# Two queues for the expert weights: the up matrices are issued by ScalarE, gates and downs by SyncE

## The chip, the cores and the metric

The kernel runs on one core of a Trainium2 chip. The metric is device time in microseconds (us), taken from the start to the end of one execution. The engines of the core are PE (TensorE, matrix products), ACT (ScalarE), DVE (VectorE), POOL (GpSimd) and SP (SyncE, which here only issues transfers). Sixteen DMA engines move data between the memory outside the core (HBM) and SBUF. An engine that issues a DMA only hands over its description; a semaphore counts up when the data have landed.

## The reference

Two layers, each a mixer (left out here: the change touches nothing of it), a layer norm, a mixture of experts, and a second layer norm, on 256 tokens of width 1024, all in float32:

```
def moe(x, router_w, router_bias, w_gate, w_up, w_down, sw_gate, sw_up, sw_down):
    ...                       # 8 of 64 experts per token, with weights wts
    def expert_block(args):
        b_tok, b_w, e = args
        xb = xt[b_tok]
        h = jax.nn.silu(xb @ w_gate[e]) * (xb @ w_up[e])
        return (h @ w_down[e]) * b_w[:, None].astype(xt.dtype)
    ...
    shared = (jax.nn.silu(xt @ sw_gate) * (xt @ sw_up)) @ sw_down
    return (routed + shared).reshape(bsz, s, d)
```

Each of the 64 experts of a layer has three matrices of 1 MB: gate and up (1024 by 256) and down (256 by 1024). Every matrix is read from HBM once per layer, 192 MB for each of the two layers.

## The kernel before

Each engine runs its own program; they meet at semaphores. The program has four stages in a row: mixer 0 (`mix0`), experts 0 (`moe0`), mixer 1, experts 1.

In a stage of experts the 64 experts are taken in 32 **pairs**. Four slots in SBUF (`ew`, `NSLOT` = 4) hold the weights of four experts, so of two pairs: the pair that is being computed and the next one. Pair n uses the slots 2u and 2u+1 with u = n mod 2; the loads for pair n+2 go into the same slots as soon as pair n has let go of them.

PE works through a pair in this order (`pe_moe`, `octets`): it waits until gate and up of both experts have landed (`gu_in`, L1119) and multiplies the gathered tokens by them (L1124, 32 products in 7.1 us; then `gu_full` counts up). It scatters the results of the pair before (L1050), turns the hidden values (L1138), gathers tokens for the next octet of experts (L1079), waits for the downs (`d_in`, L1159) and multiplies by them (L1168; then `y_hi_full` counts up). Four pairs make an octet of experts. In the last octet the gathers are replaced by products of the shared expert (L1086) and of the residual (L1067). After the last pair, L1060 scatters once more and the layer norm follows.

ACT has three tasks in a pair (`act_moe`, `octets`): SiLU of the gate half (L1388, after `gu_full`), a copy of gathered tokens (L1379, after PE's gather; PE's products L1168 wait for it), and the scaled copy of one half of the result (L1392, after `y_hi_full`). DVE does the rest.

SP issues the weights (`sp_moe`, `group`): it waits for `gu_full` of pair n, then issues gate and up of the first expert of pair n+2, gate and up of the second (L308, L309), waits for `y_hi_full` of pair n, and issues the two downs (L413). All go to SP's one queue and are served in that order. The first four experts of a layer are loaded ahead of the loop by `first_load`. After the loop, SP issues the loads of the next stage into the same queue.

Of the kernel before, what the change touches and what calls it, by code (L numbers as in the profile page):

```python
# [18 lines left out]
KC = D // P  # L19
# [4 lines left out]
NE = 64  # L24
# [62 lines left out]
def build(nc, A, out, stages=("mix0", "moe0", "mix1", "moe1")):  # L87
    ctx = ExitStack()
    with ctx:
# [212 lines left out]
                eng.wait_ge(S["h_ready"], TT * (k - 1) + t + 1)  # L302


        def expert_load(sp, m, l, e, s):
            src_g = A["exp_w_gate"][l, e].rearrange("(p c) f -> p (c f)", c=KC)
            src_u = A["exp_w_up"][l, e].rearrange("(p c) f -> p (c f)", c=KC)
            sp.dma_start(ew[:, s, 0:EW], src_g).then_inc(m["gu_in"][s], 16)  # L308
            sp.dma_start(ew[:, s, EW:2 * EW], src_u).then_inc(m["gu_in"][s], 16)  # L309

        def down_src(l, e):
            return A["exp_w_down"][l, e].rearrange("(p j) n -> p (j n)", j=JE)
# [70 lines left out]
        def sp_moe(sp, l):  # L383
# [17 lines left out]
                first_load(sp, m, l, s)  # L401
            sp_ln_params(sp, k, A["ln2_w"][l], A["ln2_b"][l])

            def group(base, it):

                for u in range(2):

                    sp.wait_ge(m["gu_full"], (base - 1) * 2 + u + 1)
                    for s in (2 * u, 2 * u + 1):
                        expert_load(sp, m, l, it * NSLOT + s, s)  # L410
                    sp.wait_ge(m["y_hi_full"], (base - 1) * 2 + u + 1)
                    for s in (2 * u, 2 * u + 1):
                        sp.dma_start(ew[:, s, 2 * EW:3 * EW], down_src(l, it * NSLOT + s)).then_inc(m["d_in"][s], 16)  # L413
# [4 lines left out]
            npass = sp.value_load(npass_i[0:1, 0:1], min_val=1, max_val=MAX_PASS)  # L418
            with sp.If(npass > 1):
                with sp.Fori(1, npass) as ps:  # L420
                    with sp.Fori(0, NE // NSLOT) as it:
                        group(ps * (NE // NSLOT) + it, it)
            return npass

# [938 lines left out]
        def act_moe(act, l, chain):  # L1363
# [18 lines left out]
            def octets(ps, it, last=False):  # L1382
                for v in range(2):
                    for q in range(OCT // 2):
                        u = q % 2
                        n = ps * PAIRS + it * OCT + v * (OCT // 2) + q
                        act.wait_ge(m["gu_full"], n + 1)
                        nc.scalar.activation(sg[:, :], bank[6][:, 0:DE], ACT.Silu).then_inc(m["silu"], 1)  # L1388
                        if not (last and v == 1):
                            gathered(1 - v, 2 * q, n + 5, 4)  # L1390
                        act.wait_ge(m["y_hi_full"], n + 1)
                        nc.scalar.activation(y_top[:, 512:1024], bank[5][:, :], ACT.Copy, scale=slot_gate[:, u:u + 1])\  # L1392
                          .then_inc(m["y_hi"], 1)
# [723 lines left out]
```

## Time and profile before

| what | us |
|---|---|
| median of 3 runs (1257.76 to 1260.94) | 1257.88 |
| the profiled execution | 1257.82 |
| its span, first to last instruction | 1256.1 |
| PE busy | 1166.2 (93% of the span) |
| ACT busy | 193.3 (15%) |
| queue q1 (SP's DMAs) | 462.37 MB, packets cover 90.5% of the time of 16 engines |
| pairs of experts 0 | from 156.32 to about 624 |
| pairs of experts 1 | from 776 to about 1244 |

Times inside the span count from its start. A busy PE says that products were in flight, and not that it ran at its peak. "DMA share" is the part of the time in which the 16 DMA engines had a packet under way; neighbouring packets overlap a little, so that it can read 1.01. "Idle before" names the event that ended an engine's idle time.

### The profile page before, as it was taken

To read this page: it belongs to the slowest core of one execution; us is meant where nothing else is said; L and a number is where in the kernel's file an instruction comes from. 1 tells how busy PE (TensorE), PEld (TensorE's weight loads), DVE (VectorE), ACT (ScalarE), POOL (GpSimd) and SP (SyncE) were. 2 spreads that over 40 slices of the span, in tenths; PEclk is the share of its full clock that TensorE was granted. 3 is DMA by queue.
4 is the path that set the end of the run, shared out by engine and by line. 5 is a ranking of instruction groups with operands and counts; after the bars stand their busy time and mean duration, and the time that the engine had idled before them with its cause. 6 is when DMAs were issued, how large, how long until landed. Compare 5 with 4: busy or idle time off the path is not lost.

```text
span 1256.1 us, 17816 instructions
## 1 busy us (share of the span) xinstructions
PE 1166.2 (93%) x7245; PEld 567.4 (45%) x7245; DVE 489.3 (39%) x1059; ACT 193.3 (15%) x330; POOL 47.3 (4%) x78
## 2 busy tenths in 40 slices
PE   9999999988888888999899999999888988889996
PEld 8774833333333333333387657333333333333332
DVE  5994733332323233332327256332333233232224
ACT  3231311111111111110122312111111111111102
POOL 6200100000000000000000001000000000000000
PEclk9999999999999999999999999999999999999999
DMA  9775989999999999999953278999999999999993
GB/s 347 205 301 193 421 344 422 420 421 421 421 421 422 422 422 422 422 421 421 399 176 134 96 288 340 419 420 422 420 421 422 420 422 422 422 422 421 421 422 154
DMA packets 76125, 463.78 MB, mean 369 GB/s; under 512 B 8544, under 2 KB 9888, under 8 KB 25376
## 3 DMA queue, kind: packets, MB, share of 16 engines
q1 hardware_dynamic: 75920, 462.37, 90.5%
q8 instruction: 47, 0.77, 0.2%
q10 hardware_dynamic: 144, 0.52, 0.1%
q14 instruction: 14, 0.11, 0.0%
HBM read 456.51 MB, written 6.36 MB: 368 GB/s over the span
## 4 chain that ended last, share of the span: by engine, by line
PE 51%; DMA 42%; SPq 3%; DVE 2%; issue 1%; ACT 1%; DVEq 0%; POOL 0%; POOLq 0%
DMA expert_weights<-in_exp_w_up 40%; PE bank L1124 23%; PE bank L1168 5%; PE bank L652 4%; PE bank L638 3%; PE bank L999 2%; PE bank L726 2%; PE bank L742 2%; SPq L308 2%; PE bank L1050 1%; PE bank L753 1%; DMA expert_weights<-s_rows 1%; PE bank L1079 1%; SPq L309 1%; DMA s_rows<-hidden 1%
## 5 line engine op out<-in xcount | busy, mean ns | idle before, releaser
L1124 PE MATMUL bank<-expert_weights,weight_ring 128*64 128x512 f32 x1024 | 226.8, 595 | 30.9 <-DMA expert_weights<-in_exp_w_up 30.9
L1168 PE MATMUL bank<-expert_weights,hiddenT 128*32 128x512 f32 x2048 | 233.0, 595 | 10.0 <-ACT weight_ring L1379 5.0
L1989 DVE TENSOR_TENSOR hidden<-silu_gate,bank 128x256 f32<-128x256 f32 x64 | 27.0, 422 | 424.3 <-ACT silu_gate L1388 424.3
L1124 PEld LDWEIGHTS bank<-expert_weights,weight_ring 128*64 128x64 f32 x1024 | 81.1, 137 | 175.5 <-issue 175.2
L1124 PE MATMUL bank<-expert_weights,hT 128*64 128x512 f32 x512 | 118.4, 603 | 30.7 <-DMA expert_weights<-in_exp_w_up 30.4
L1168 PEld LDWEIGHTS bank<-expert_weights,hiddenT 128*32 128x32 f32 x2048 | 60.0, 109 | 146.0 <-issue 119.4
L1124 PE MATMUL bank<-expert_weights,octet_high 128*64 128x512 f32 x512 | 116.0, 592 | 0.0
L1388 ACT ACTIVATE silu_gate<-bank 128x256 f32<-128x256 f32 x64 | 24.6, 385 | 471.1 <-PE bank L1124 471.1
L2001 DVE TENSOR_SCALAR y_top<-bank,slot_gate 128x512 fp32r<-128x512 f32 x64 | 48.1, 751 | 108.1 <-PE bank L1168 108.1
L1124 PEld LDWEIGHTS bank<-expert_weights,hT 128*64 128x64 f32 x512 | 39.5, 138 | 110.1 <-issue 110.1
L1392 ACT ACTIVATE y_top<-bank,slot_gate 128x512 fp32r<-128x512 f32 x64 | 44.0, 687 | 268.7 <-PE bank L1168 268.7
L1124 PEld LDWEIGHTS bank<-expert_weights,octet_high 128*64 128x64 f32 x512 | 42.6, 137 | 67.2 <-issue 67.2
L2008 DVE SCALAR_TENSOR_TENSOR y_low<-bank,slot_gate,y_top 128x512 fp32r<-128x512 f32 x64 | 48.0, 751 | 57.6 <-ACT y_top L1392 57.6
L1079 PE MATMUL bank<-onehot_r,h_top 128*128 128x256 f32 x256 | 67.8, 300 | 0.0
L638 PE MATMUL bank<-hT,weight_ring 128*128 128x256 f32 x304 | 66.6, 380 | 0.0
L1079 PE MATMUL bank<-onehot_r,h_low 128*128 128x256 f32 x256 | 62.7, 279 | 0.0
L638 PEld LDWEIGHTS bank<-hT,weight_ring 128*128 128x128 f32 x304 | 57.4, 190 | 7.8
L1050 PE MATMUL bank<-y_top,onehotT_r 64*128 64x512 f32 x256 | 57.5, 445 | 0.0
L652 PE MATMUL bank<-weight_ring,hT 128*128 128x512 f32 x128 | 56.2, 594 | 0.1
L1050 PE MATMUL bank<-y_low,onehotT_r 64*128 64x512 f32 x256 | 50.5, 390 | 0.0
L2004 DVE SCALAR_TENSOR_TENSOR y_low<-bank,slot_gate,y_top 128x512 fp32r<-128x512 f32 x64 | 48.1, 751 | 2.3
L1079 PEld LDWEIGHTS bank<-onehot_r,h_top 128*128 128x128 f32 x256 | 48.8, 191 | 0.0
(384 smaller groups left out, 1061.5 us busy)
## 6 DMA issues: line engine op xcount, KB each, us to landing
expert_weights<-in_exp_w_gate SPq DMA_DIRECT2D x128, 1024.0 KB, 15.0
expert_weights<-in_exp_w_up SPq DMA_DIRECT2D x128, 1024.0 KB, 17.1
expert_weights<-in_exp_w_down SPq DMA_DIRECT2D x128, 1024.0 KB, 18.7
weight_ring<-in_w_in_even SPq DMA_DIRECT2D x5, 2048.0 KB, 9.9
weight_ring<-in_w_out SPq DMA_DIRECT2D x4, 2048.0 KB, 7.8
weight_ring<-in_w_in_odd SPq DMA_DIRECT2D x4, 2048.0 KB, 10.5
s_c<-expert_weights SPq DMA_DIRECT2D x1, 3072.0 KB, 9.7
expert_weights<-s_c SPq DMA_DIRECT2D x1, 3072.0 KB, 10.3
```

The costliest lines, as they stand in the source:

```text
L308: sp.dma_start(ew[:, s, 0:EW], src_g).then_inc(m["gu_in"][s], 16)
L638: last = nc.tensor.matmul(B.tile(f"{name}{i}")[:, a * SEQ:(a + 1) * SEQ], w[:, c, (2 * i + a) * P:(2 * i + a + 1) * P], hT[:, c, :], start ...
L652: last = nc.tensor.matmul(B.tile(f"{name}{t}")[:, :], hT[:, c, t * P:(t + 1) * P], w[:, c, :], start=(c == 0), stop=(c == KC - 1))
L1050: nc.tensor.matmul(bank[2 * t + n][:, :], onehotT[slot_rows(t), par, :], part[slot_rows(t), n * 512:(n + 1) * 512], start=False, stop=Fals ...
L1079: last = nc.tensor.matmul(bank[b][:, t * SEQ:(t + 1) * SEQ], part[:, t, c, :], onehot[:, t, :, :].rearrange("p e s -> p (e s)"), start=(pa ...
L1124: last_mm = nc.tensor.matmul(bank[6][a * 2 * CAP:(a + 1) * 2 * CAP, :].rearrange("p (w f) -> p w f", w=2), octet_tokens(l, v, c)[:, 2 * q ...
L1168: last_mm = nc.tensor.matmul(bank[b][by_tile:by_tile + CAP, :], hm[:, j, own:own + CAP], ew_d(2 * u + a)[:, j, half * 512:(half + 1) * 512 ...
L1392: nc.scalar.activation(y_top[:, 512:1024], bank[5][:, :], ACT.Copy, scale=slot_gate[:, u:u + 1])\
L1989: nc.vector.tensor_tensor(hslot[:, :], sg[:, :], bank[6][:, DE:2 * DE], ALU.mult)\
L2001: nc.vector.tensor_scalar(y_top[:, 0:512], bank[4][:, :], slot_gate[:, u:u + 1], None, ALU.mult)\
L2004: nc.vector.scalar_tensor_tensor(out=y_low[:, 0:512], in0=bank[4][:, :], scalar=slot_gate[:, u:u + 1], in1=y_top[:, 0:512], op0=ALU.mult, ...
L2008: nc.vector.scalar_tensor_tensor(out=y_low[:, 512:1024], in0=bank[5][:, :], scalar=slot_gate[:, u:u + 1], in1=y_top[:, 512:1024], op0=ALU. ...
```

## The change

`expert_load` gets a switch for its second transfer, and in the loop SP leaves the ups out. ACT issues them itself: right after its SiLU of pair n it issues the two ups of pair n+2, on its own DMA queue. The semaphores stay the same: `gu_in` of a slot still counts 16 for the gate and 16 for the up, and PE still waits for both. The first four experts of a layer are still loaded whole by SP. Further passes over the experts, which only other inputs would need, keep their first group whole as well.

```
-        def expert_load(sp, m, l, e, s):
+        def expert_load(sp, m, l, e, s, with_up=True):
             src_g = A["exp_w_gate"][l, e].rearrange("(p c) f -> p (c f)", c=KC)
             src_u = A["exp_w_up"][l, e].rearrange("(p c) f -> p (c f)", c=KC)
             sp.dma_start(ew[:, s, 0:EW], src_g).then_inc(m["gu_in"][s], 16)
-            sp.dma_start(ew[:, s, EW:2 * EW], src_u).then_inc(m["gu_in"][s], 16)
+            if with_up:
+                sp.dma_start(ew[:, s, EW:2 * EW], src_u).then_inc(m["gu_in"][s], 16)
...
-            def group(base, it):
+            def group(base, it, with_up=False):
...
-                        expert_load(sp, m, l, it * NSLOT + s, s)
+                        expert_load(sp, m, l, it * NSLOT + s, s, with_up)
...
                         act.wait_ge(m["gu_full"], n + 1)
                         nc.scalar.activation(sg[:, :], bank[6][:, 0:DE], ACT.Silu).then_inc(m["silu"], 1)
+                        if not (last and v == 1 and q >= 2):
+                            for a in range(2):
+                                up = A["exp_w_up"][l, it * 2 * OCT + v * OCT + 2 * q + NSLOT + a]
+                                act.dma_start(ew[:, 2 * u + a, EW:2 * EW], up.rearrange("(p c) f -> p (c f)", c=KC))\
+                                   .then_inc(m["gu_in"][2 * u + a], 16)
                         if not (last and v == 1):
                             gathered(1 - v, 2 * q, n + 5, 4)
```

SP's loop over the pairs of experts 0, before, for one pair (ISA and REGISTER_ALU compute addresses; the names are destination and source of a transfer):

```order
L308 ISA [waits moe0_gu_full]
L308 DMA expert_weights<-in_exp_w_gate 128x2048
L309 DMA expert_weights<-in_exp_w_up 128x2048
L308 ISA
L308 DMA expert_weights<-in_exp_w_gate 128x2048
L309 DMA expert_weights<-in_exp_w_up 128x2048
L413 DMA expert_weights<-in_exp_w_down 128x2048 [waits moe0_y_hi_full]
L413 DMA expert_weights<-in_exp_w_down 128x2048
```

The same place on SP now:

```order
L308 ISA [waits moe0_gu_full]
L308 DMA expert_weights<-in_exp_w_gate 128x2048
L308 ISA
L308 DMA expert_weights<-in_exp_w_gate 128x2048
L414 DMA expert_weights<-in_exp_w_down 128x2048 [waits moe0_y_hi_full]
L414 DMA expert_weights<-in_exp_w_down 128x2048
```

The two ups are gone from between the gates; waits and the rest stand as they did.

ACT at the first two pairs of experts 1, before:

```order
L1388 ACTIVATE silu_gate<-bank 128x256 [waits moe1_gu_full]
L1378 REGISTER_ALU
L1379 COPY hT<-bank 128x2x8x32 [waits moe1_gather_lo]
L1392 ACTIVATE y_top<-bank,slot_gate 128x512 [waits moe1_y_hi_full]
L1388 ACTIVATE silu_gate<-bank 128x256 [waits moe1_gu_full]
```

The same place on ACT now:

```order
L1390 ACTIVATE silu_gate<-bank 128x256 [waits moe1_gu_full]
L1394 DMA expert_weights<-in_exp_w_up 128x2048 x2
L1380 REGISTER_ALU
L1381 COPY hT<-bank 128x2x8x32 [waits moe1_gather_lo]
L1399 ACTIVATE y_top<-bank,slot_gate 128x512 [waits moe1_y_hi_full]
L1390 ACTIVATE silu_gate<-bank 128x256 [waits moe1_gu_full]
```

The two issues stand between SiLU and the copy of gathered tokens and bring no wait of their own. ACT does this for 30 of the 32 pairs of a layer; the last two have nothing more to load.

## Rows read from the trace of the kernel before

**Rows 1.** Page, DMA by 40 slices of the span, and the queues.

```profile
DMA  9775989999999999999953278999999999999993
GB/s 347 205 301 193 421 344 422 420 421 421 421 421 422 422 422 422 422 421 421 399 176 134 96 288 340 419 420 422 420 421 422 420 422 422 422 422 421 421 422 154
...
q1 hardware_dynamic: 75920, 462.37, 90.5%
```

**Rows 2.** Windows in the expert stages: engines' busy us, clock, DMA share, GB/s.

```profile
core 0: us, PE busy (x) PEld busy (x) DVE busy (x) ACT busy (x) POOL busy (x), PEclk, DMA share, GB/s
166.00:176.00 10.00, 9.82 (x62) 3.15 (x64) 3.14 (x5) 0.81 (x2) 0.00 (x0) 1.00 1.01 428
176.00:184.00 8.00, 7.78 (x59) 3.23 (x57) 3.43 (x7) 1.66 (x3) 0.00 (x0) 1.00 1.01 418
200.00:350.00 150.00, 137.91 (x860) 56.80 (x857) 46.34 (x94) 16.97 (x31) 0.00 (x0) 1.00 1.01 421
1000.00:1200.00 200.00, 181.53 (x1122) 75.36 (x1122) 60.15 (x124) 21.55 (x39) 0.00 (x0) 1.00 1.01 422
```

**Rows 3.** Waits over the span, then SP's own: us in total, times, longest.

```profile
PE bank L1124 <- DMA expert_weights<-in_exp_w_up: 61.3, 45, 2.6
...
SPq L308 <- PE bank L1124: 450.9, 60, 24.1
```

**Rows 4.** Timeline of a middle pair: PE, then ACT, then SP.

```profile
311.59 7.09 PE L1124 MATMUL bank<-expert_weights,weight_ring 128*64 128x512 f32 x32 [1.41 <-DMA expert_weights<-in_exp_w_up]
321.45 3.64 PE L1168 MATMUL bank<-expert_weights,hiddenT 128*32 128x512 f32 x32 [0.20 <-ACT octet_high L1379]
326.48 3.65 PE L1124 MATMUL bank<-expert_weights,hT 128*64 128x512 f32 x16 [1.39 <-DMA expert_weights<-in_exp_w_up]
...
318.72 0.39 ACT L1388 ACTIVATE silu_gate<-bank 128x256 f32<-128x256 f32 x1 [7.78 <-PE bank L1124]
320.81 0.59 ACT L1379 COPY octet_high<-bank 128x512 f32<-128x512 f32 x1 [1.71 <-PE bank L1079]
...
318.86 0.33 SPq L308 DMA_DIRECT2D expert_weights<-in_exp_w_gate  x1
319.28 0.38 SPq L309 DMA_DIRECT2D expert_weights<-in_exp_w_up  x1
```

**Rows 5.** Source views of L309 (up) and L308 (gate): issue ns, landing us.

```profile
L309 SPq DMA_DIRECT2D expert_weights<-in_exp_w_up x128: 352/382/792, 119.2 to 1210.3; - x128
DMA to landing us min/median/max: 6.9/17.1/23.5
...
DMA to landing us min/median/max: 4.9/15.0/21.5
```

**Rows 6.** Timeline of the start: the only DMA that ACT issues.

```profile
0.81 0.43 ACTq L1439 DMA_DIRECT2D weight_ring<-in_w_first  x1
```

**Rows 7.** DMA view of 2.5 to 4.5 us: both queues, packets, MB, share.

```profile
DMA packets 256, 0.79 MB, mean 395 GB/s; under 512 B 103, under 2 KB 103, under 8 KB 223
...
q10 hardware_dynamic: 135, 0.49, 61.9%
q1 hardware_dynamic: 121, 0.30, 40.0%
```

**Rows 8.** Timeline of PE, last four pairs of experts 0: start, length, idle before.

```profile
566.56 3.65 PE L1124 MATMUL bank<-expert_weights,hT 128*64 128x512 f32 x16 [0.82 <-DMA expert_weights<-in_exp_w_up]
581.46 3.65 PE L1124 MATMUL bank<-expert_weights,hT 128*64 128x512 f32 x16
596.41 3.65 PE L1124 MATMUL bank<-expert_weights,hT 128*64 128x512 f32 x16
611.44 3.65 PE L1124 MATMUL bank<-expert_weights,hT 128*64 128x512 f32 x16 [1.02 <-DMA expert_weights<-in_exp_w_up]
```

**Rows 9.** The same of experts 1.

```profile
1186.77 3.65 PE L1124 MATMUL bank<-expert_weights,hT 128*64 128x512 f32 x16 [1.16 <-DMA expert_weights<-in_exp_w_up]
1201.56 3.65 PE L1124 MATMUL bank<-expert_weights,hT 128*64 128x512 f32 x16
1216.41 3.65 PE L1124 MATMUL bank<-expert_weights,hT 128*64 128x512 f32 x16
1231.31 3.65 PE L1124 MATMUL bank<-expert_weights,hT 128*64 128x512 f32 x16 [0.89 <-DMA expert_weights<-in_exp_w_up]
```

More of the change, by code:

```diff
@@ L420, in sp_moe @@
                 with sp.Fori(1, npass) as ps:
-                    with sp.Fori(0, NE // NSLOT) as it:
+                    group(ps * (NE // NSLOT), 0, True)
+                    with sp.Fori(1, NE // NSLOT) as it:
                         group(ps * (NE // NSLOT) + it, it)
```

## The prediction

> **What bounds the kernel now.** I read the page's DMA slices first. Through both expert stages the digit is 9, and 28 of the 40 slices stand at 419 to 422 GB/s [rows 1]. The windows say the same in a sharper way: over 150 us of the first expert stage and 200 us of the second the DMA share is 1.01, at 421 and 422 GB/s, while PE is busy 92% and 91% of the time at clock 1.00 [rows 2]. So the DMA engines have no gap there, and PE has some. The waits agree: PE stood 61.3 us in 45 pieces before L1124, all put down to a landing up, at most 2.6 us at once [rows 3]. One middle pair shows the cadence: PE starts L1124 at 311.59 and again at 326.48, so a pair takes 14.89 us, and each start had waited some 1.4 us for the last up [rows 4]. The arithmetic fits: a pair is 6 MB, or 6.29 million bytes, and that at 421 GB/s is 14.9 us. I call a third of it (two gates, two ups or two downs) a **piece** of 4.97 us. The stage is bounded by bytes; the number of issues does not bound it.
>
> SP is no bound. It stood 450.9 us in 60 waits for `gu_full` [rows 3], and what it issues lies in the queue for long: an up lands 17.1 us after its issue in the median, and 6.9 us at least [rows 5].
>
> **The change part by part.**
>
> *SP loses two issues a pair*, 0.38 us each [rows 5], 120 in all. SP waits right afterwards in any case, so this is worth nothing.
>
> *ACT gains two issues a pair.* The trace has one DMA issued by ACT, 0.43 us [rows 6]; SP's ups took 0.35 to 0.79 [rows 5]. ACT has 2.09 us from the start of SiLU (318.72) to the copy L1379 (320.81), SiLU needs 0.39 of it, and 1.71 are idle [rows 4]. Two issues at 0.43 make 0.9 us and fit; even two at 0.79 make 1.6 us and fit. If they did not, the copy would be late, then L1168, and then PE's 1.4 us of waiting before the next pair would have to cover it [rows 4]. I take 0. In the last octet the copy is gone and no cover is needed.
>
> *The bytes stay*, and the first gate of a layer goes out at the same moment as before. With the engines full from there on, the last byte of a layer lands when it did, unless the rate changes. That is the largest open item, since the trace has no stretch in which two queues of large packets are both full. Its bounds are from the nearest rows: 428 GB/s when the stream has just begun and 418 shortly after, against 421 in the long run [rows 2], so +1.7% and -0.7%. I take 0: the share is already 1.01, so there is no bubble between packets for a second queue to fill.
>
> *The order of service changes*, and this is the term that I expect to see. Before, one queue gave gates and ups of pair n, downs of n, gates and ups of n+1, and so on. Now SP's queue holds gates n, downs n, gates n+1, and ACT's holds ups alone. In the only stretch with two queues, both move packets in the same two microseconds, 135 and 121 of them [rows 7]. So they take turns; what share each gets with equal packets this does not settle, and I take half and half. Then the ups run ahead of the gates, which stand behind the downs. How far ahead? Let T be the moment when gates and ups of pair n are both there. Before, everything up to ups n had been served at T. Now gates n come last; everything up to gates n has been served, and on top of it a part of ups n+1. As the engines never rest, T is later by exactly the time of that part.
>
> Ups n+1 are handed over 7.13 us after PE starts pair n-1 (311.59 to 318.72) and a further 0.6 us for SiLU and the issue, so 7.7 us after it [rows 4]. A transfer that nothing stood before took 4.9 us to land [rows 5], of which 2.49 are its 1 MB, so 2.4 us lie around the bytes. Gates n land 0.1 us before PE starts pair n, 14.89 us after the start of n-1. That leaves 14.89 - 7.7 - 2.4 - 0.1 = 4.7 us in which both queues are full, and at half of the turns 2.3 us of ups n+1 are served in it. **T is 2.3 us late**, with 0 and 4.7 us as the ends (no turn, and every turn, for ACT's queue).
>
> In the middle of a stage this costs nothing, as the engines go on. At its end it does: after the last pair there are no ups to run ahead, so the last T is where it was, but PE has to get there. Its last four pairs hardly wait. In experts 0 they start at 566.56, 581.46, 596.41 and 611.44; only the last had waited, 1.02 us [rows 8]. In experts 1 the last had waited 0.89 us and the two before it had no wait [rows 9]. A lateness of 2.3 us at the first of the four goes through all, less that wait: 2.3 - 1.02 = 1.3 us, and 2.3 - 0.89 = 1.4 us. **Sum: +2.7 us**, with ends 0 and (4.7 - 1.02) + (4.7 - 0.89) = 7.5 us.
>
> The downs come later too, but not too late: downs n follow gates n with 4.97 us of their own and share turns with what is left of ups n+1, 2.7 us, so they land 7.7 us after T, and L1168 wants them 9.86 us after the start (311.59 to 321.45) [rows 4]. Cover 2.2 us.
>
> The profiled execution took 1257.82 us, 1.7 more than its span and 0.1 less than the median of the three runs, so the sum can be put on either: 1257.8 + 2.7 = **1260.5 us**.
>
> The Trainium skill (*DMA: Bandwidth & Descriptors*, Queues, rings and completion order) says that each DMA engine goes round its queues packet by packet. The trace agrees as far as it goes, with 135 and 121 packets side by side [rows 7]; by that rule the half is right and the sum is the one above.
>
> **The rivals.** About 0.3% (3.8 us) is what a measurement of this kernel can tell from no change.
>
> *The order stays.* If the engines took the packets roughly as they were issued, or SP's queue got most turns, T would be late by less than 1.02 and 0.89 us, and the waits of the last pair would swallow that: 1257.8 us. For it: ups still go out within a microsecond of the gates. Against it: ACT's queue has no downs in it, so its ups stand at its head while the gates still wait. It decides from about a fifth of the turns downwards.
>
> The same page of the Trainium skill (Issuing engines are not separate DMA queues) holds that issuing from several engines saves no more than issue time. By that rule, too, the time stays at 1257.8 us, SP's issue time being off the path. The full DMA share of 1.01 agrees with it as far as bandwidth goes; the order of service it leaves out.
>
> *Slower: the engines lose by alternating.* Each packet would be followed by one of another matrix. Both queues are full for the 9.9 us that a piece takes at half rate, so two thirds of 60 x 14.9 = 894 us, 596 us. At the lower bound of 0.7% [rows 2] this is 4.2 us, and 1257.8 + 2.7 + 4.2 = 1264.7 us. It decides from (3.8 - 2.7) / 596 = 0.2%. For it: the rate fell from 428 to 418 within 10 us, once several transfers were queued. Against it: from there it came back to 421 with the same queue.
>
> *Faster: a second queue restores 428 GB/s* in these 596 us: 1.7% of it is 10 us, 1257.8 + 2.7 - 10 = 1250.5 us. For it: the trace shows that rate as an opening state [rows 2]. Against it: nothing in the trace ties it to the number of queues.
>
> *ACT's issues are long.* With more than 0.85 us each the copy L1379 is late, but it would take a further 1.4 us before a pair gets longer. I see no row for that.
>
> **How the numbers follow.** Forecast 0.42 (1260.5; with more turns for ACT's queue up to 1265, and I put 0.06 of this case over 3.8 us). Order stays 0.19 (1257.8). Alternating costs 0.25 (1264.7). Second queue gains 0.12 (1250.5). Long issues 0.02 (over 1262). So faster 0.12, within 0.3% 0.55, slower 0.33. For the range I leave out the far half of the gain and the far end of the loss, about 0.2 together: 1253 to 1266.5.
>
> **What would show it.** Right: a second queue in the page with 120 ups, some 126 MB; DMA share 1.01 and 421 GB/s as before in the middle of the stages; PE's waits before L1124 now put down to gates and not to ups; ups that land well before their gates; the last pair of each stage without a wait of PE; both stages 1 to 2 us longer. ACT's copy L1379 still waits for PE. Wrong: a rate other than 421 by 0.2% or more, DMA share under 1.00 in the middle, waits of PE before L1168 for downs, or waits for ups as they were (the order stayed).

## The result, and the profile after

The changed kernel takes 1260.42 us (median of 20 runs, 1258.83 to 1262.35), the kernel before 1258.26 us on the same chip (20 runs, 1257.23 to 1260.94). The ratio is 1.0017, with a 95% interval of 1.0010 to 1.0023: 2.2 us slower. The interval leaves out "no change", although the single runs of the two kernels overlap, and it stays under 0.3%. The profiled execution has a span of 1258.2 us (before 1256.1). The new lines move the numbers: the gate and up products L1124 are L1126 now, the down products L1168 are L1170, SiLU L1388 is L1390, ACT's copy L1379 is L1381, its new issue L1394 and its result copy L1399 (before L1392).

The page, answering to [rows 1]: rate by 40 slices, the two queues, and the chain that ended last by engine.

```profile
GB/s 346 205 301 198 422 340 423 420 421 422 420 421 421 422 422 422 421 421 421 385 171 132 96 288 347 421 420 421 421 421 421 421 421 422 422 422 420 421 421 142
...
q1 hardware_dynamic: 58640, 336.53, 66.1%
q10 hardware_dynamic: 17424, 126.36, 24.3%
...
PE 67%; DMA 30%; ACT 1%; DVE 1%; issue 1%; ACTq 0%; SPq 0%; DVEq 0%; POOL 0%; POOLq 0%
```

Windows of the expert stages, as in [rows 2]: busy us of the engines, granted clock, DMA share, GB/s.

```profile
166.00:176.00 10.00, 10.00 (x62) 3.11 (x64) 2.94 (x5) 0.69 (x1) 0.00 (x0) 1.00 1.00 424
176.00:184.00 8.00, 7.79 (x61) 3.38 (x59) 3.61 (x8) 1.66 (x3) 0.00 (x0) 1.00 1.01 396
200.00:350.00 150.00, 139.20 (x848) 55.96 (x844) 45.87 (x93) 16.57 (x30) 0.00 (x0) 0.98 1.01 421
1000.00:1200.00 200.00, 188.85 (x1124) 75.20 (x1121) 60.16 (x123) 21.93 (x40) 0.00 (x0) 0.97 1.01 421
```

126 MB have gone to the second queue, and the rate in the middle of both stages is 421 GB/s at a share of 1.01 (421 and 422 in [rows 2]). So the change took nothing from the transfers as a whole and gave them nothing. What differs there is the granted clock, 0.98 and 0.97 where it was 1.00, and PE's busy time. In the chain that ended last, PE has 67% and DMA 30%; before it was 51% and 42%: more pairs now start without a wait for weights, because PE is still behind.

PE's waits for gates and ups, as in [rows 3]: us in total, times, longest.

```profile
PE bank L1126 <- DMA expert_weights<-in_exp_w_up: 33.2, 19, 4.1
PE bank L1126 <- DMA expert_weights<-in_exp_w_gate: 13.0, 6, 2.7
```

There are 25 waits of up to 4.1 us, where before there were 45 of up to 2.6: the pairs come unevenly now. The names "gate" and "up" say nothing here. Both matrices of an expert count up one semaphore, and in all 120 cases (two matrices a pair, 60 pairs) the profile gives the earlier landing to the one that was issued first. From pair 10 to pair 25 SP issues its gate at the same moment as ACT its up or up to 0.05 us ahead, in the other pairs ACT is ahead by 0.13 us or more, and so the names swap. What can be counted is the packets of each queue, 256 of 8 KB for the two matrices of a pair: by them the ups of a pair are served before its gates in 57 of the 60 pairs, pairs 10 to 25 included. T, the later of the landings, does not depend on the names.

Timeline of ACT around a middle pair, as in [rows 4]: SiLU, the two new issues, the copy.

```profile
306.23 0.39 ACT L1390 ACTIVATE silu_gate<-bank 128x256 f32<-128x256 f32 x1 [6.31 <-PE bank L1126]
306.37 0.90 ACTq L1394 DMA_DIRECT2D expert_weights<-in_exp_w_up  x2
308.32 0.59 ACT L1381 COPY octet_high<-bank 128x512 f32<-128x512 f32 x1 [1.70 <-PE bank L1081]
```

The copy still waits 1.70 us for PE (1.71 before): the two issues, 0.90 us together, lie within ACT's idle time.

Whether the queues take turns, which the opening of the kernel had to stand for [rows 7], the changed kernel shows itself. The DMA view of 312 to 318 us, with weights waiting in both queues: packets, MB, share.

```profile
q10 hardware_dynamic: 172, 1.28, 51.6%
q1 hardware_dynamic: 171, 1.23, 49.7%
```

As many packets of the one as of the other. And the ends of the stages, PE's last four pairs in experts 0, answering to [rows 8], then in experts 1, answering to [rows 9]:

```profile
568.88 3.65 PE L1126 MATMUL bank<-expert_weights,hT 128*64 128x512 f32 x16 [1.42 <-DMA expert_weights<-in_exp_w_gate]
...
583.67 3.65 PE L1126 MATMUL bank<-expert_weights,hT 128*64 128x512 f32 x16
...
598.57 3.65 PE L1126 MATMUL bank<-expert_weights,hT 128*64 128x512 f32 x16
...
612.51 3.65 PE L1126 MATMUL bank<-expert_weights,hT 128*64 128x512 f32 x16
...
1189.82 3.65 PE L1126 MATMUL bank<-expert_weights,hT 128*64 128x512 f32 x16 [1.45 <-DMA expert_weights<-in_exp_w_gate]
...
1204.61 3.65 PE L1126 MATMUL bank<-expert_weights,hT 128*64 128x512 f32 x16
...
1219.47 3.65 PE L1126 MATMUL bank<-expert_weights,hT 128*64 128x512 f32 x16
...
1233.40 3.65 PE L1126 MATMUL bank<-expert_weights,hT 128*64 128x512 f32 x16
```

The first of the four waits for its gates and starts late. The others follow without a wait, the last included, which before had waited 1.02 and 0.89 us. Its weights were there 1.0 us before PE came to it. This is where the time went.

To compare kernels whose stages start at different times, a stage is measured from the start of its first SiLU to the start of ACT's last result copy, mixer 1 from there to the first SiLU of experts 1, and the stream from the first SiLU to the landing of the last downs (all in us, read from the timelines). T of a pair is the moment when its gates and ups are there, counted from the first SiLU.

| kernel | stage 0 | mixer 1 | stage 1 | stream 0, 1 | T of pair 28 | T of pair 31 | start of pair 31 |
|---|---|---|---|---|---|---|---|
| before | 460.82 | 158.96 | 460.89 | 452.69, 452.85 | 402.98, 403.40 | 447.85, 447.95 | 447.99, 448.08 |
| before, second trace | 461.03 | 158.78 | 460.83 | 452.91, 452.79 | 403.12, 403.11 | 448.08, 447.86 | 448.22, 448.00 |
| after | 462.11 | 159.25 | 461.64 | 453.38, 452.71 | 405.52, 405.10 | 448.25, 447.80 | 449.28, 448.81 |
| after, second trace | 461.89 | 158.95 | 462.29 | 453.20, 453.15 | 405.41, 405.18 | 448.00, 448.24 | 449.06, 449.46 |

The second traces are the two unchanged kernels profiled once more:

> The kernel before, unchanged, for a second trace: mixer 1 (from the end of experts 0 to the first gate product of experts 1), which was 158.96 us in the first trace, is the same within 0.2 us if the longer mixers of the kernels whose ScalarE issues transfers belong to these kernels, and differs by up to 1 us if mixers scatter from run to run.

> The changed kernel, unchanged, for a second trace: by theory A the gates and ups of pair 28 of each layer are again complete some 2 us later than in the kernel before (2.5 and 1.7 us in the first trace) and each stage ends 0.7 to 1.5 us later; by the theory that the first trace was chance, the lateness is gone or changes sign. Mixer 1 was 159.24 us in the first trace; it stays within 0.2 us of that if the extra belongs to the kernel.

They took 1259.52 and 1260.15 us. Pair 28 is late by 2.54 and 1.70 us in the first traces, by 2.29 and 2.07 in the second. The stages are longer by 1.29 and 0.75, and by 0.86 and 1.46: 1.1 us on average each. T of pair 31 moves by 0.1 on average, and the streams by 0.7 us in 453 at most. Mixer 1 scatters by 0.3 us in the kernel after, so its first trace (+0.3) alone shows no effect of the change (more on mixer 1 in the last section). The second trace of before starts its experts 1.7 us later than the first for no reason in the program, which is what a single trace's span can hide.

### The profile page after: what moved, and what is told of

Its sections match the earlier page's. It is cut to its first block, busy times and chain, and to the rows that moved or that the text cites. A ratio compares the mean times of both kernels' runs of the same rounds, so it can differ in the third digit from the quotient of the medians.

```text
span 1258.2 us, 17826 instructions
## 1 busy us (share of the span) xinstructions
PE 1184.3 (94%) x7245; PEld 564.8 (45%) x7245; DVE 489.4 (39%) x1059; ACT 193.4 (15%) x330; POOL 47.1 (4%) x78
## 4 chain that ended last, share of the span: by engine, by line
PE 67%; DMA 30%; ACT 1%; DVE 1%; issue 1%; ACTq 0%; SPq 0%; DVEq 0%; POOL 0%; POOLq 0%
PE bank L1126 28%; DMA expert_weights<-in_exp_w_up 19%; DMA expert_weights<-in_exp_w_gate 10%; PE bank L1170 9%; PE bank L640 5%; PE bank L654 4%; PE bank L1052 3%; PE bank L1001 2%; PE bank L728 2%; PE bank L744 2%; PE bank L1081 2%; PE bank L755 1%; PE bank L1088 1%; PE bank L1074 1%; PE bank L1140 1%
## 5 line engine op out<-in xcount | busy, mean ns | idle before, releaser
L1126 PE MATMUL bank<-expert_weights,weight_ring 128*64 128x512 f32 x1024 | 235.2, 613 | 19.7 <-DMA expert_weights<-in_exp_w_up 14.7
L1170 PE MATMUL bank<-expert_weights,hiddenT 128*32 128x512 f32 x2048 | 233.0, 595 | 10.0 <-ACT weight_ring L1381 5.0
L1126 PEld LDWEIGHTS bank<-expert_weights,weight_ring 128*64 128x64 f32 x1024 | 78.3, 140 | 174.6 <-issue 174.4
L1126 PE MATMUL bank<-expert_weights,hT 128*64 128x512 f32 x512 | 128.6, 647 | 26.7 <-DMA expert_weights<-in_exp_w_up 18.6
L1170 PEld LDWEIGHTS bank<-expert_weights,hiddenT 128*32 128x32 f32 x2048 | 60.0, 109 | 146.0 <-issue 119.4
L1126 PE MATMUL bank<-expert_weights,octet_high 128*64 128x512 f32 x512 | 115.8, 592 | 0.0
L1390 ACT ACTIVATE silu_gate<-bank 128x256 f32<-128x256 f32 x64 | 24.6, 384 | 473.3 <-PE bank L1126 473.3
L1126 PEld LDWEIGHTS bank<-expert_weights,hT 128*64 128x64 f32 x512 | 40.8, 147 | 114.2 <-issue 114.2
L1399 ACT ACTIVATE y_top<-bank,slot_gate 128x512 fp32r<-128x512 f32 x64 | 44.0, 687 | 268.7 <-PE bank L1170 268.7
L1126 PEld LDWEIGHTS bank<-expert_weights,octet_high 128*64 128x64 f32 x512 | 40.7, 137 | 69.4 <-issue 69.4
## 6 DMA issues: line engine op xcount, KB each, us to landing
expert_weights<-in_exp_w_gate SPq DMA_DIRECT2D x128, 1024.0 KB, 14.1
weight_ring<-in_w_in_odd SPq DMA_DIRECT2D x4, 2048.0 KB, 10.2
```

What stands on the lines that cost most here:

```text
L1126: last_mm = nc.tensor.matmul(bank[6][a * 2 * CAP:(a + 1) * 2 * CAP, :].rearrange("p (w f) -> p w f", w=2), octet_tokens(l, v, c)[:, 2 * q ...
L1170: last_mm = nc.tensor.matmul(bank[b][by_tile:by_tile + CAP, :], hm[:, j, own:own + CAP], ew_d(2 * u + a)[:, j, half * 512:(half + 1) * 512 ...
```

## Experiments

Three theories were to be told apart. **A**: the rate is untouched; the second queue changes the order in which bytes are served, gates and ups of a pair are complete some 2 us later, and this costs time only where PE must catch up behind the last weights, at the two ends. **B**: two queues move the bytes more slowly (0.2% of the stages would do). **C**: ACT's issues, or the program that ACT then runs, cost the time.

### Ups of the last six pairs of each layer back on SP's queue (x1)

```diff
-                        if not (last and v == 1 and q >= 2):
+                        if not last:
-            with sp.Fori(1, NE // NSLOT) as it:
+            with sp.Fori(1, 13) as it:
                 group(it, it)
+            with sp.Fori(13, NE // NSLOT) as it:
+                group(it, it, True)
```

> The changed kernel, but the ups of the last six pairs of each layer go back to SP's queue, between the gates; ACT issues the 24 before them. Theory A (the order of service makes the last four pairs late, and PE cannot catch up): with the order of before restored ahead of them the cost is gone, 0 us against before, within 0.8 us; the last pair of each stage waits about 1 us for its weights again. Theory B (the engines lose rate by alternating between two queues): 24 of 30 pairs still alternate, so four fifths of 2.2 us stay, +1.7 us. Theory C (ACT's two issues delay its copy and so PE): the issues stay in 24 of 30 pairs, +1.7 us.

It took 1258.54 us, ratio 0.9998 (0.9989 to 1.0007). The change stands in most pairs of each layer, and once the end is as before the time shows no cost. Timeline of the last pair of experts 0 (the products' line is L1130 here):

```profile
611.67 3.65 PE L1130 MATMUL bank<-expert_weights,hT 128*64 128x512 f32 x16 [1.46 <-DMA expert_weights<-in_exp_w_up]
```

The last pair waits for its weights again. Theories B and C, by which 24 of the 30 pairs of the loop should still pay, fall for the better part of the loss. T of pair 28 is 403.00 and 403.63 us, as in the kernel before (402.98 and 403.40). The stages were still 0.5 us longer than in the first trace of before. The two traces of before differ by 0.2 us in experts 0 and by 0.1 in experts 1, so 0.3 to 0.5 us a stage stay open.

### Ups issued later, behind the result copy (x2, x8)

ACT issues the ups beside the downs rather than beside the gates, so that the gates are not overtaken. In x2 the first pair of a layer keeps its early ups, in x8 the first four (there the condition ends at `v == 0`).

```diff
-                        if not (last and v == 1 and q >= 2):
+                        if first and v == 0 and q == 0:
                             for a in range(2):
                                 up = A["exp_w_up"][...]
...
                         act.wait_ge(m["y_hi_full"], n + 1)
...
+                        if not (last and v == 1 and q >= 2) and not (first and v == 0 and q == 0):
+                            for a in range(2):
+                                up = A["exp_w_up"][...]
```

> The changed kernel, but ACT issues the ups after its last task of a pair (the scaled copy of the result) and not after SiLU, some 6.5 us later; only the first pair of a layer keeps the early place, so that the stream of weights starts as before. Two queues alternate as much as in the changed kernel. Theory A: the ups can no longer run ahead of the gates by more than their own pair, so the gates land when they did before: 0 us against before, within 0.8 us. Theory B: the alternation is the same, +2.2 us. Theory C: the issues no longer stand ahead of the copy that PE waits for, 0 us.

It took 1260.05 us, ratio 1.0017 (1.0007 to 1.0026), against the expectation. The start of the stage shows why. Window of 180 to 190 us, and PE's start of pair 3:

```profile
180.00:190.00 10.00, 10.00 (x64) 2.98 (x56) 2.56 (x5) 0.69 (x1) 0.00 (x0) 1.00 0.96 380
```

```profile
198.55 7.09 PE L1126 MATMUL bank<-expert_weights,weight_ring 128*64 128x512 f32 x32 [1.89 <-DMA expert_weights<-in_exp_w_up]
```

The loop had not filled its queues yet when the ups came 6 us later than before, so the DMA engines ran dry (share 0.96, 380 GB/s, where the kernel before has 1.01 and 418), and pair 3 waited 1.89 us. In experts 1, where the stage became 2.6 us longer, the stretch from 829 to 839 us has a share of 0.98 and 386 GB/s, and the stream is 455.43 us, 2.6 longer. This is a loss of its own, not the one under study. With the first four pairs early it should go:

> x2_late_ups again, but the first four pairs of a layer keep the early place of the ups. In x2_late_ups the stream of weights ran dry between the second and the third pair (DMA share 0.96 from 180 to 190 us), and experts 1 got 2.6 us longer. Theory A: with the stream full from the start, gates run no longer late; what stays is the end, where the last ups are handed over together with the last downs and share turns with them, some 0.7 us a layer: +0.5 to +1.5 us against before, and the DMA stream as long as before. Theory B (rate lost by alternating): +2.2 us, and a stream that is 1 us longer in each stage.

It took 1259.02 us, ratio 1.0006 (0.9997 to 1.0015), and the streams were 452.68 and 452.84 us, as in the kernel before. Two queues with 126 MB on the second thus move the bytes at the old rate; B falls. T of pair 28 is 402.95 and 403.75, within 0.4 us of before: with ups that no longer run ahead, the lateness of some 2 us is gone. That late ups cost nothing is not shown: the stages were 461.71 and 461.95 us, 0.9 and 1.1 longer than in the first trace of before, and T of pair 31 is 448.76 and 449.00, later by as much. The last ups are handed over together with the last downs there and take turns with them, which would make T late at the very end; no run separates this.

### The downs on ACT's queue instead of the ups (x3)

If overtaking is the cause, a second queue that runs ahead with 2 MB that nobody needs yet must cost more. Here SP issues gates and ups, and ACT the downs behind its result copy.

```diff
-                        if not (last and v == 1 and q >= 2):
-                            for a in range(2):
-                                up = A["exp_w_up"][...]
...
+                        if not (last and v == 1 and q >= 2):
+                            for a in range(2):
+                                act.dma_start(ew[:, 2 * u + a, 2 * EW:3 * EW],
+                                              down_src(l, it * 2 * OCT + v * OCT + 2 * q + NSLOT + a))
```

> Gates and ups stay with SP in their old order, and ACT issues the downs, after the scaled copy of the result. SP waits for the last downs before it starts on the next stage's weights, so that these stay behind them as before. Theory A: downs of a pair now share turns with gates and ups of the same pair and run ahead of them almost whole, so a pair's gates and ups are complete up to a piece of 4.97 us later, at the last pair too: +4 to +5 us a layer, +8 to +10 us in all. Theory B: two queues alternate for two thirds of the stream, as in the changed kernel, +2.2 us. Theory C: ACT's issues stand behind its copy, 0 us.

It took 1268.47 us, ratio 1.0080 (1.0067 to 1.0093): 10.2 us slower with the same bytes, the same two queues and the same engine that issues. The streams are 452.97 and 452.50 us, within 0.4 us of before, and yet the stages are 4.9 and 5.3 us longer. T of pair 31 is 452.72 and 453.24, later by 4.9 and 5.3 us. That is the time which the last pair's two downs take (2 MB at 421 GB/s, 5.0 us): they are served along with its gates and ups instead of after them. The last downs land 0.3 us after T of pair 31 in experts 0 and 0.7 us before it in experts 1; in the kernel before they landed 4.8 and 4.9 us after it. SP's hold before the next stage adds nothing here: mixer 1 is 159.12 us. The last pair waits for its gates and ups (0.92 us in experts 0):

```profile
615.78 3.65 PE L1130 MATMUL bank<-expert_weights,hT 128*64 128x512 f32 x16 [0.92 <-DMA expert_weights<-in_exp_w_up]
```

### Everything on ACT's one queue (x4, x7)

ACT issues gates and ups behind SiLU and downs behind its result copy, so there is one order again, and ACT has six issues a pair, not two. In x4, SP holds back the loads of the next stage until the last downs have landed; in x7 ACT issues the first of these itself (the last two lines).

```diff
-                                act.dma_start(ew[:, 2 * u + a, EW:2 * EW], up.rearrange("(p c) f -> p (c f)", c=KC))\
-                                   .then_inc(m["gu_in"][2 * u + a], 16)
+                                e = it * 2 * OCT + v * OCT + 2 * q + NSLOT + a
+                                expert_load(act, m, l, e, 2 * u + a)
...
+                        if l == 0 and last and v == 1 and q == 1:
+                            ring_load(act, ring_no["u1"])
```

> All weights of the loop are issued by ACT on its one queue, gates and ups after SiLU, downs after the scaled copy, in the order that SP had; SP issues none of them (and waits for the last downs before it starts on the next stage). One queue, the order of before, and twice the issues ahead of ACT's copy: four at some 0.45 us are 1.8 us and SiLU 0.4 us, against 2.1 us from SiLU to the copy. Theory A: 0 us, within 0.8 us. Theory B: 0 us. Theory C: the issues cost, twice as much as in the changed kernel, +4 us.

It took 1262.42 us, ratio 1.0028 (1.0017 to 1.0039). The total is what C expected, the place is not: the stages are 0.2 and 0.3 us longer than in the first trace of before, and mixer 1 is 163.00 us instead of 158.96. Its first products wait for a transfer of 3 MB that lands in the weight slots (`s_c`). The rows of that transfer (KB, us from issue to landing) and of SP, in x4:

```profile
expert_weights<-s_c SPq DMA_DIRECT2D x1, 3072.0 KB, 14.7
```

```profile
617.49 0.56 SPq L277 DMA_DIRECT2D weight_ring<-in_w_in_odd  x1
619.88 0.34 SPq L365 DMA_DIRECT2D expert_weights<-s_c  x1
```

SP's wait had put the load of `in_w_in_odd` 19 us later (598.41 in the kernel before), right ahead of `s_c`, which therefore landed at 634.6 and not at 628.9. With that load where it was:

> x4_all_act again, all weights of the loop on ACT's one queue in the old order, but without SP's wait: ACT issues the next mixer's first weights behind the last downs, as SP did. In x4_all_act both expert stages took only 0.2 to 0.3 us longer than before, and mixer 1 took 4 us longer, where SP had held back these weights. Theory A: 0 to +0.6 us against before. Theory C (ACT's issues cost): still +4 us.

It took 1258.80 us, ratio 1.0000 (0.9991 to 1.0009), with stages of 461.61 and 460.86. Three times as many issues from ACT cost nothing that can be measured (the interval is 1.1 us to either side, and C asked for 4); C falls.

### The last pairs without the work that fills PE (x5, x6)

In the last pairs PE has more products (shared expert, residual), because of which, by theory A, it cannot catch up. The expectations count ten a layer; the kernel has twelve: one in each of pairs 24 to 27, three in each of 28 and 29, two in 30. x5 is the changed kernel without them, x6 the kernel before without them; they leave out this part of the result.

```diff
-                        if last and v == 0:
-                            shared_down(0, q // 2, q % 2)
-                        if ending and q < 2:
-                            shared_down(1, q, 0)
-                            shared_down(1, q, 1)
-                            add_alpha_h(q, 0)
-                        if ending and q == 2:
-                            add_alpha_h(0, 1)
-                            add_alpha_h(1, 1)
```

> The changed kernel without the ten products a layer that the last octet carries for the shared expert (L1088) and the residual (L1069), so a part of the sum is missing; this takes 2 to 3 us each out of PE's pairs 28 and 29 and 1.9 us out of pair 30. Theory A (lateness that PE cannot make up in the last pairs): now PE can make it up, the last pair waits for its weights again and starts when they land: 0 us against the kernel before with the same products left out (x6_before_cut), within 0.8 us, though pair 28 still starts some 2 us late. Theory B (the engines lose rate in the whole stage): the last byte is late, so the 2.2 us stay. Theory C (ACT's issues cost): the 2.2 us stay as far as they fall in the last four pairs, where ACT has no copy; no clear number.

> The kernel before without the same ten products a layer (a part of the sum is missing): the control for x5_after_cut. The last pair starts when its weights land, which does not change; the products after it are the same. All theories: 0 us against before, within 0.5 us.

x6 took 1258.29 us (1.0002, 0.9993 to 1.0011): before, these products are hidden. x5 took 1260.24 us (1.0015, 1.0006 to 1.0025), so the loss of the changed kernel did not go away, against A. Experts 0 did as A says: T of pair 31 is 447.76, PE starts it 0.13 us later, and the stage is 460.72 us. In experts 1 the stage is 462.54. Timeline of PE there, pairs 30 and 31:

```profile
1219.33 4.99 PE L1126 MATMUL bank<-expert_weights,hT 128*64 128x512 f32 x16 [3.31 <-DMA expert_weights<-in_exp_w_gate]
1224.14 3.61 PE L1126 MATMUL bank<-expert_weights,octet_high 128*64 128x512 f32 x16
...
1233.67 3.65 PE L1126 MATMUL bank<-expert_weights,hT 128*64 128x512 f32 x16
```

Pair 30 starts behind a wait of 3.31 us, and its first 16 products take 4.99 us instead of 3.65. The granted clock in that stretch (windows, PE alone):

```profile
1216.00:1219.30 3.30, 0.02 (x3) 0.90 1.04 432
1219.30:1221.00 1.70, 1.67 (x4) 0.50 0.98 410
1221.00:1223.00 2.00, 2.00 (x10) 0.73 1.07 434
1223.00:1228.00 5.00, 5.00 (x26) 1.00 1.00 415
```

While PE waits, the clock falls to the lower of its two levels (0.50 is 1.2 GHz), and it comes back some 3 us after PE has begun again. This makes pair 30 later, and pair 31 starts 1.74 us behind its weights. So the unevenness that the second queue brings can cost at the end in another way as well: not because PE is full, but because it had to wait long and then ran slowly. In the changed kernel itself this has no part in the ends: in both of its traces the gate and up products of the last four pairs take 7.12 to 7.13 us, as before. Mixer 1 is 160.10 us in this trace, 1.1 longer than before (see the last section).

### Shorter ends (x9, x12)

If each stage hangs on PE's last pairs behind the last weights, the end can be shortened without any second queue. x9 is the kernel before, with the twelve products moved to pairs 4 to 7, and with gates and ups of the last eight pairs of each layer (the expectation says four) loaded in two halves of the contraction, so that PE starts a pair on its first half and waits for the second half way.

```diff
+        def expert_halves(sp, m, l, e, slots):
+            n = EW // 2
+            for x, name in ((0, "gu_in"), (1, "gu_half")):
+                for a, s in enumerate(slots):
+                    for w, src in ((0, A["exp_w_gate"]), (1, A["exp_w_up"])):
+                        flat = src[l, e + a].rearrange("(p c) f -> p (c f)", c=KC)
+                        sp.dma_start(ew[:, s, w * EW + x * n:w * EW + (x + 1) * n], flat[:, x * n:(x + 1) * n])\
+                          .then_inc(m[name][s // 2 if x else s], 16)
...
                         for c in range(KC):
+                            if last and c == KC // 2:
+                                pe.wait_ge(m["gu_half"][u], ...)
...
-                        if last and v == 0:
+                        if first and v == 1:
                             shared_down(0, q // 2, q % 2)
```

> The kernel before, in which the end of each expert stage is shortened without touching the queue: the ten products of the shared down and the residual go from the last eight experts to the first eight, and the gates and ups of the last four pairs of each layer are loaded as two halves of the contraction, each with a semaphore of its own, so that TensorE can begin a pair on its first half. Theory A (the ends of the stages hang on TensorE's last pairs behind the last weights): the last pair starts some 3 to 5 us before its last bytes land instead of after them, which shortens each stage by up to 3.5 us (half of the pair's 7.1 us of gate and up products); with 0 to 3.5 us a layer the time is 1251 to 1258, most likely near 1252. If the stage's end is set by the stream alone (last downs' landing), or the halves (4 KB a row instead of 8 KB) move more slowly, it is 1258 or more.

It took 1259.67 us, ratio 1.0013 (1.0004 to 1.0022): a miss. The last pairs do overlap with their weights, but the halves move more slowly. Windows of x9, whole matrices, then halves:

```profile
440.00:500.00 60.00, 53.58 (x336) 22.64 (x337) 18.23 (x37) 6.63 (x12) 0.00 (x0) 1.00 1.01 420
520.00:600.00 80.00, 69.50 (x419) 25.73 (x417) 19.98 (x41) 7.12 (x13) 0.00 (x0) 1.00 1.02 413
```

Rows of 4 KB instead of 8 came at 413 GB/s; in the same stretch the kernel before moved 421. The streams are 455.24 and 456.07 us, longer by 2.6 and 3.2, and the stages shorter by only 1.11 and 0.29. And what experts 0 gained, mixer 1 gave back and more: it took 163.29 us, since its first products again had to wait for `s_c`, which stood behind the late downs and landed 14.1 us after its issue, at 631.1 (before: 10.3 us, at 628.9). In the kernel before, mixer 1's first products started at 629.61, so experts 0 can gain less than a microsecond before the last byte decides; only behind experts 1 does no such transfer stand. For x12 the halves are kept to the last two pairs of experts 1.

> Like the kernel with halves in four pairs of each layer's end and more, but in experts 1 alone and for its last two pairs alone, since in that run the halves cost some 0.4 us of transfer a pair (the stage's last downs landed 456.07 us after the first SiLU instead of 452.85, with eight pairs in halves), and since experts 0 gives what it gains back to mixer 1, whose first products wait for a transfer that lands behind the downs. Theory A (the end of a stage hangs on TensorE's last pairs behind the last weights): TensorE has 1.4 us to spare a pair once the ten products stand elsewhere, so pair 30 starts 1.4 and pair 31 2.8 us ahead of its last bytes; less 0.8 us for four matrices a pair in halves the stage is 2.0 us shorter, 458.9 instead of 460.9, and the time 1256.2 (0 to -2.8 us). If the last downs set the end instead, the stage is 0.8 us longer and the time 1259.0.

It took **1255.11 us** (1254.62 to 1255.86), before 1258.54 in the same rounds, ratio 0.9972 (0.9962 to 0.9983), faster than both kernels. Stage 1 is 458.05 us, 2.84 shorter, with a stream only 0.7 longer. Timeline of PE in the last pair of experts 1, first half and second:

```profile
1227.29 3.65 PE L1145 MATMUL bank<-expert_weights,hT 128*64 128x512 f32 x16
1231.75 3.65 PE L1145 MATMUL bank<-expert_weights,octet_high 128*64 128x512 f32 x16 [0.81 <-DMA expert_weights<-in_exp_w_up]
```

PE works through the first half while the second is still on its way, and waits 0.81 us for it; in the last pair of [rows 9] all 32 products began at the last landing. The moved products have no part in the gain as far as x6 goes, where leaving them out changed nothing. That the end of experts 1 is set by PE behind the last gates and ups, on which the prediction's sum rests, is shown by this from the other side.

## Why the prediction was right, point by point

- **SP's and ACT's issues at no cost**: right. The copy waited 1.70 us for PE as before, and with all issues on ACT (x7) the time was that of the kernel before. The longest single issue was 1.27 us, the median 0.36, two of them 0.90 together, within the cover of 1.71.
- **Bytes and rate at 0, within +1.7% and -0.7%**: right, and the bounds were far too wide. The rate was 421 in the middle, and the streams differ by at most 0.7 us in 453. The 424 and 396 GB/s at the start of experts 0 (before 428 and 418) are some 0.5 us of bytes, an estimate from these windows; they may be the better part of the 0.7 us in that trace. The last T moved by 0.4 us there, and by 0.1 on average over the four stages.
- **Turns half and half**: right. 172 and 171 packets in the same 6 us; between 200 and 600 us, in the 269 microseconds in which both queues moved more than 8 packets of 8 KB, 6983 of SP's and 6814 of ACT's.
- **T late by 2.3 us**: right at the pair that counts. Measured 2.54, 1.70, 2.29 and 2.07 at pair 28, on average 2.15. The constant lateness that the prediction worked with is not what the middle of a stage shows: in pairs 6 to 27 T swings between 0.9 us earlier and 3.0 us later than before, on average 1.0 to 1.8 later by stage and trace. The prediction's formula takes the pair before as being on time; a pair that starts late hands over its ups late, so that less of them is served ahead of the next gates. That this makes the swing is argued and not shown. Nor does the prediction give a reason why pair 28, on which its sum rests, was among the late ones in all four stages.
- **+1.3 and +1.4 at the ends**: right in kind, a quarter of a microsecond too large on average, with a scatter that the sum did not have: 1.29 and 0.75 in the first traces, 0.86 and 1.46 in the second, 1.1 each. The last T stayed where it was (+0.1 on average), and PE came to it 1.0 to 1.2 us late, as the sum said. The scatter is that of T in pairs 28 and 29, less the waits that the last four pairs had before; the granted clock is not in it. For 2.7 us of forecast, 2.2 were measured. x5 bears the condition out in experts 0, where the loss went with the products that fill PE, and shows in experts 1 what the prediction does not speak of: behind a long wait the granted clock can make the last pair late although PE is not full.
- **Cover of the downs, 2.2 us**: right. There is no wait of PE before L1170 for downs. Counted with the prediction's 9.86 us, the downs of pair 28 of experts 0 landed 2.2 us before L1170 wanted them; the least in the two traces was 0.4 us, at a pair whose T was hardly late (pair 14 of experts 1).
- **What would show it**: the second queue, share, rate, last pairs and copy as said. The stages are longer by 0.75 to 1.46 us, two of the four just under the 1 us that was named. The naming of PE's waits came out mixed (19 for ups, 6 for gates); the signature was badly chosen, since with a shared semaphore the name follows the order of issue alone. By the packets the ups are there first, as it said.
- **The rivals**: "the order stays" fell with T, and with x3. "The engines lose by alternating" and "a second queue restores 428" fell with the streams, most clearly in x8. "ACT's issues are long" fell with x7. The Trainium skill (*DMA: Bandwidth & Descriptors*, Issuing engines are not separate DMA queues) says that issuing from several engines saves only the issue time. The streams agree as far as bandwidth goes; the time does not, by 2.2 us with the ups and 10.2 us with the downs on the second queue, through the order of service.

That the median came out within 0.1 us of the forecast is luck: the sum was 0.5 us too large (2.7 for 2.2), and the median of three runs on which it was put was 0.4 us under that of the twenty. A single trace of either kernel moves each stage by up to 0.7 us.

## What to carry to other kernels

A second DMA queue is first of all a change of order: with both queues full, each got half of the packets here, whatever was needed first. Where transfers set the pace that cost nothing in the middle of a stage; look at the last pieces, at what is served ahead of them, and at whether the engine behind them has slack to catch up. To gain time there, let the consumer start on a part of the last piece, but split only the last pieces, and look first at what the next stage waits for: a gain is given back where the next stage hangs on the last byte.

## What the runs showed of the hardware

**The granted clock fell behind long waits of PE.** With T swinging, some of PE's waits before a pair became longer, and behind most of the long ones it ran at the lower level for a while: behind 21 of the 28 waits of more than 2 us in the two traces after. After, pair 6 of experts 0, first the two groups of 16 products, then the windows of the wait and of what follows (PE alone):

```profile
239.55 5.35 PE L1126 MATMUL bank<-expert_weights,hT 128*64 128x512 f32 x16 [2.72 <-DMA expert_weights<-in_exp_w_gate]
244.70 3.63 PE L1126 MATMUL bank<-expert_weights,octet_high 128*64 128x512 f32 x16
```

```profile
236.80:239.50 2.70, 0.04 (x4) 1.00 1.03 428
239.50:242.00 2.50, 2.45 (x8) 0.58 1.01 419
242.00:244.00 2.00, 2.00 (x10) 0.67 1.01 414
244.00:248.00 4.00, 4.00 (x22) 1.00 1.01 420
```

The clock is still full in the wait, then 0.58 and 0.67 (a mix of the two levels, 1.2 and 2.4 GHz) for some 4 us of work. The pair's products take 8.82 us from start to SiLU instead of 7.13. This befell 12 of the 64 pairs in the first trace after, 9 in the second, and one and two in the two traces before. In the middle of a stage the transfers hide it.

The same clock goes with mixer 1's scatter. Its first 64 products follow a wait of 2.6 us, and they run from 629.61 to 633.55 in the kernel before and from 630.66 to 635.51 after, 0.9 us longer, with these windows, before and then after:

```profile
632.00:634.00 2.00, 1.65 (x25) 0.92 0.84 270
```

```profile
632.00:634.00 2.00, 2.00 (x28) 0.50 0.92 212
```

In six traces (after, x1, x2, x5, x7, x8) these products take 4.85 us, all of it at the lower level, and mixer 1 is 159.24 to 160.10 us; in six others (before twice, the second trace after, x3, x6, x12) they take 3.94 to 4.26 us, and mixer 1 is 158.71 to 159.12. In x4 and x9 mixer 1 waits for `s_c`. All six long ones are kernels in which ACT issues weights, and none of the four traces without is among them (before twice, x6, x12); whether the second issuer has a part in it no run shows.

**Half rows cost 2% of the rate**: 413 instead of 421 GB/s at 4 KB a row. Whether it is the length of the rows or the doubled number of transfers no run here tells apart.

What stays open: what makes the six long mixers differ by 0.9 us among themselves, why T swings, and the last microsecond of x8's stages.
